# Value columns of two dilated groups by one product of 512 columns, and w_out's second read asked for later

## The chip, the cores and the metric

The kernel runs on one NeuronCore of a Trainium2 chip, as one launch. The metric is the device time of that launch in microseconds (us), the median of a few executions; lower is better. Engines are named as the profile names them: PE is TensorE's matmul, PEld its weight load, DVE VectorE, ACT ScalarE, POOL GpSimd, SP SyncE, which here only asks for transfers. Everything is in float32 unless it says bf16.

## The reference, cut to what matters

One layer of a hybrid decoder for a prompt of 512 tokens and eight sample tokens. The normalised input is multiplied by one wide weight w_in (1024 x 4992), and the columns of the product go to three kinds of heads:

```python
u = rmsnorm(x, norm_mix)                       # (512, 1024) and (8, 1024)
cols = split(u @ w_in, COL_SIZES)              # 4992 columns
aq, af, ai, ag, bq, bk, bv = cols[:7]          # 384 columns each: recurrence (a), differential attention (b)
dil = [cols[7+3*g : 10+3*g] for g in range(3)] # q, k, v of 256 columns for each dilated group
mix = concat(hgrn2(aq, af, ai, ag), diff_attention(bq, bk, bv), combine(dilated(dil, rates=(1, 4, 16))))
h = x + mix @ w_out
h = h + moe(rmsnorm(h))                        # top group of 4, two of its 4 experts
y = rmsnorm(h + sigmoid(rmsnorm(h) @ pgw) * (p @ ppw))
```

In groups 1 and 2 a token attends to tokens 4 or 16 places apart, so their values are wanted in an order in which the tokens with the same remainder modulo 4 stand together.

## The kernel before

The input, transposed, lies in `xT`: 128 partitions x 8 blocks of the 1024 features x 520 tokens. w_in is read in 13 slabs of 384 columns (1.5 MB each) into two buffers in the tile `EXPERT`, in the order of the constant `ORDER` (0, 1, 2, 4, 5, 6, 7, 9, 11, 8, 3, 10, 12). Slab 10 is the twelfth and lies in buffer 1, slab 12 is the last and lies in buffer 0. `projection_units` cuts every slab into units. A unit is one accumulation over the 8 feature blocks into one of two PSUM banks, which take turns (`ps[:, u % 2]`), and a copy by ACT:

- FM ("feature major"): 128 columns of w_in are the weights of the array, 512 tokens stream through: 8 products of 512 columns (L2184).
- TM ("token major"): 128 tokens of `xT` are the weights, the slab's columns stream through: 384 of them for slabs 2, 3 and 6, 256 for the values in slabs 8, 10 and 12 (L2189). For slabs 10 and 12 `cols` picks every fourth token, so the weights are read from `xT` with a step of four elements.
- SM: the slab's 384 columns for the eight sample tokens (L2195).

A float32 product shows as two records, here called passes: 8 products are 16 passes. `schedule` cuts each unit into four pieces, of two feature blocks and so four passes each (32 for SM), and writes one list of steps that all engines walk through in the same order, each doing its part. From slab 7 on the pieces are woven into the differential attention as work for PE between its steps: 24 rounds n (6 heads in each of 4 blocks of queries), with `d_s(n)` (scores), `d_t(n-1)` (transposes) and `d_pv(n-2)` (times values), and 1.7 pieces behind every step. Between them a round passes through DVE and ACT: DVE takes the largest score (L1645), ACT the exponentials of two maps (L1176), DVE weighs them (`weigh`, L1657 to L1660), then PE transposes (L2282), ACT copies (L1186) and PE multiplies by the values (L2294). On DVE's list `weigh(n-1)` stands ahead of the maximum of round n. Between the rounds also stand work for the sample tokens (`dec_q`, `dec_new` on DVE) and the gates (`gate_fn` and others). After the rounds the dilated attention begins with `c_s(0)` (L2312, L2314; maximum L1668), with `mtp(0, .)` and `dec_soft` behind it, and the first product by w_out, `wop(0, 0, 0)` (L2459).

SP asks for all transfers in list order: a slab is asked for when the slab two before it has been used up (`load_slab`, L730). w_out is read in three parts. Part 1 (rows 3 to 5 of 8, 1.5 MB) goes into slab buffer 1 and was asked for once slab 10 was used up; part 0 (rows 0 to 2) goes into buffer 0 and is asked for when all units are done and part 1 has landed; part 2 comes later. `wop(0, 0, 0)` waits for part 1, `wop(0, 0, 1)` for part 0 as well. `cached(b, kv)` reads pages of the cache, and waits until DVE has used the buffer; `outputs` stores values; `reload` reads rows of x again.

The mixture of experts then reads 48 weight blocks of 2 MB through nine slots, and the last part is the per-layer input gate (L2732).

Of the kernel before, what the change touches and what calls it, by code (L numbers as in the profile page):

```python
# [15 lines left out]
ACT = mybir.ActivationFunctionType  # L16
AX = mybir.AxisListType

P = 128
D = 1024  # L20
DC = D // P
SEQ = 512
NT = SEQ // P
# [3 lines left out]
SLAB = 384  # L27
NSLAB = N_IN // SLAB
# [49 lines left out]
ORDER = (0, 1, 2, 4, 5, 6, 7, 9, 11, 8, 3, 10, 12)  # L78
# [5 lines left out]
def projection_units():  # L84

    units = []
    for s in ORDER:
        col = s * SLAB
        if s < 7:
            kinds = ("FM", "FM", "TM", "TM", "FM", "FM", "TM")[s]  # L90
            if kinds == "FM":
                units += [("FM", s, c * P, P, (s, c)) for c in range(3)]
            else:
                units += [("TM", s, 0, SLAB, (s, i)) for i in range(NT)]
        else:
            g, half = divmod(col - C_COL, 768)
            if half == 0:
                units += [("FM", s, c * P, P, (7 + g, c)) for c in range(3)]
            else:
                units += [("FM", s, 0, P, (7 + g, 3))]  # L100
                units += [("TM", s, P, 2 * P, (7 + g, i)) for i in range(NT)]

        units.append(("SM", s, 0, SLAB, None))
        units[-1], units[-2] = units[-2], units[-1]
    return units


def unit_marks(units):

    last = {sl: max(u for u in range(len(units)) if units[u][1] == sl) for sl in range(NSLAB)}  # L110
    summed = {units[u][1]: u for u in range(len(units)) if units[u][0] == "SM"}
    return last, summed
# [14 lines left out]
def schedule(units):  # L127

    last, summed = unit_marks(units)
# [3 lines left out]
    def project_one():  # L133
        u, c0, c1 = todo.pop(0)
        steps.append(("proj", u, c0, c1))
        at = ORDER.index(units[u][1])
        if u == last[units[u][1]] and c1 == DC and at == NSLAB - 2:
            steps.append(("w_out_load", 1))
        if u == last[units[u][1]] and c1 == DC and at + 2 < NSLAB:
            steps.append(("slab", at + 2))  # L140
            if at < 8:
                steps.extend([("copy", 1 + x, at) for x in range(2)])
            elif at < 10:
                steps.extend([("copy", 0, 4 * (at - 8) + x) for x in range(4)])
# [55 lines left out]
    c = []  # L200
# [13 lines left out]
    stop = len(units)  # L214
# [129 lines left out]
def hybrid_kernel(nc, a, o):  # L344
    ctx = ExitStack()
    with ctx:
        def sb(name, shape, dt=F32):
            return ctx.enter_context(nc.sbuf_tensor(name, shape, dt))
# [9 lines left out]
        EXPERT = sb("EXPERT", [P, 2 * CAPW])  # L358
# [10 lines left out]
        cvT = EXPERT[:, at0:at0 + NT * NG * 256].rearrange("p (g i n) -> p g i n", g=NG, i=NT)  # L369
# [15 lines left out]
        xT = sb("xT", [P, DC, NTOK])  # L385
# [28 lines left out]
        ps = ctx.enter_context(nc.psum_tensor("ps", [P, 8, 512], F32))  # L414
# [81 lines left out]
        S_ = {n: sem(n) for n in names}  # L496
# [127 lines left out]
        NU = len(UNITS)  # L624
        LASTU, SUMU = unit_marks(UNITS)
# [14 lines left out]
        def cols(ap):  # L640
            return ap.rearrange("p (s r) -> p r s", r=4)
# [72 lines left out]
        def _(sp):  # L714
            for i in range(NT + 1):
                src = a["x_prompt"][0, i * P:(i + 1) * P, :] if i < NT else a["x_sample"].rearrange("b t d -> (b t) d")
# [84 lines left out]

            def w_out_load(part):
                if part == 1:
                    sp.wait_ge(S_["unit_pe"], 1 + LASTU[ORDER[NSLAB - 2]])
                    dst, src = EXPERT[:, 3 * D:6 * D], wo[:, 3:6]
                elif part == 0:
                    sp.wait_ge(S_["unit_pe"], NU)
                    sp.wait_ge(S_["woload"], 16)
                    dst, src = EXPERT[:, 0:3 * D], wo[:, 0:3]
                else:  # L810
                    sp.wait_ge(S_["c_s_pe"], NCU // 2)
                    sp.wait_ge(S_["kr_pe"], SOFT_KR)
                    dst, src = EXPERT[:, 8 * D:10 * D], wo[:, 6:8]
                sp.dma_start(dst.rearrange("p (c n) -> p c n", n=D), src).then_inc(S_["woload"], 16)
# [96 lines left out]
            for i in range(T5):  # L911
                src = a["p_prompt"][0, 0, i * P:(i + 1) * P, :] if i < NT else a["p_sample"][0].rearrange("b t d -> (b t) d")
# [132 lines left out]
        def _(act):  # L1045
            n = [0]
            s = nc.scalar
# [31 lines left out]
            def proj(u, k0, k1):  # L1079
                kind, sl, c0, w, at = UNITS[u]  # L1080
                if k1 < DC:
                    return
                act.wait_ge(S_["unit_pe"], u + 1)
                src = ps[:, u % 2, :]
                scale = 1.0
                if kind == "TM" and at == (2, 0):
                    act.wait_ge(S_["tab_ok"], 1)
                if kind == "FM" and at == (9, 0):
                    act.wait_ge(S_["s_o_pe"], 1)
                if kind == "SM":  # L1090
                    for q in range(4):
                        at_ = sl * SLAB + q * QSL
                        last = s.activation(samp[:, at_:at_ + QSL], src[32 * q:32 * q + NS, 0:QSL], ACT.Copy)
                    last.then_inc(S_["unit_ok"], 1)
                    return
                elif kind == "TM":
                    g, i = at
                    dst = iT[:, i] if g == 2 else gT[:, i] if g == 3 else bvT[:, i] if g == 6 else cvT[:, g - 7, i]
                    src = src[:, 0:w]
                else:  # L1100
                    g, c = at
                    if g < 2:
                        dst = aF[:, g, c, 0:SEQ]
                    elif g < 7:
                        dst, scale = dF[:, g - 4, c], SCALE_B if g == 4 else 1.0
                    else:
                        dst, scale = cF[:, g - 7, c], SCALE_C if c < 2 else 1.0
                        if g > 7:
                            dst, src = dst.rearrange("p (r s) -> p r s", r=4), cols(src)
                s.activation(dst, src, ACT.Copy, scale=scale).then_inc(S_["unit_ok"], 1)  # L1110
# [1046 lines left out]
        def _(pe):  # L2157
            t = nc.tensor
# [3 lines left out]
            for i in range(NT + 1):  # L2162
# [4 lines left out]
                for c in range(DC):  # L2167
                    last = t.transpose(ps[:, 2 + 2 * (i % 2) + c // 4, (c % 4) * P:(c % 4) * P + r],
                                       XM[0:r, i, c * P:(c + 1) * P], ident[0:r, 0:r])
                last.then_inc(S_["xt_pe"], 1)  # L2170
            pe.wait_ge(S_["xt_ok"], 2 * NT)

            def proj(u, k0, k1):
                kind, sl, c0, w, at = UNITS[u]
                at_ = ORDER.index(sl)
                W_ = slab[at_ % 2]
                if k0 == 0:
                    pe.wait_ge(slabload[at_ % 2], 16 * (at_ // 2 + 1))
                if k0 == 0 and u >= 2:

                    pe.wait_ge(S_["unit_ok"], u - 1)
                for c in range(k0, k1):
                    if kind == "FM":
                        last = t.matmul(ps[:, u % 2, :], W_[:, c, c0:c0 + w], xT[:, c, 0:SEQ],  # L2184
                                        start=(c == 0), stop=(c == DC - 1))
                    elif kind == "TM":
                        i = at[1]
                        rows_ = cols(xT[:, c, 0:SEQ])[:, i] if at[0] > 7 else xT[:, c, i * P:(i + 1) * P]
                        last = t.matmul(ps[:, u % 2, 0:w], rows_,  # L2189
                                        W_[:, c, c0:c0 + w], start=(c == 0), stop=(c == DC - 1))  # L2190
                    elif kind == "SM":
                        if u == SUMU[ORDER[0]] and c == 0:
                            pe.wait_ge(S_["xt_ok"], 2 * (NT + 1) + 1)
                        for q in range(4):
                            last = t.matmul(ps[32 * q:32 * q + 32, u % 2, 0:QSL], xS[:, c, :],  # L2195
                                            W_[:, c, q * QSL:(q + 1) * QSL], start=(c == 0), stop=(c == DC - 1))
                if k1 == DC:
                    last.then_inc(S_["unit_pe"], 1)
# [381 lines left out]
            for k in range(T5):  # L2580
                last = t.matmul(ps[:, 6, T5 * NE:(T5 + 1) * NE], onesb, C[:, k], start=(k == 0), stop=(k == T5 - 1))
            last.then_inc(S_["rank_pe"], 1)
            pe.wait_ge(S_["rank_ok"], 1)
            for i in range(T5):
                for k in range(2):
                    last = t.matmul(ps[:, 2, 0:1], R0[:, i], partsb[:, i, k:k + 1], start=(i + k == 0), stop=(i + k == T5))
# [75 lines left out]
            for m in range(2 * T5):  # L2662
                for k in range(2):
                    last = t.matmul(ps[:, 6, 96:96 + MAXT], Rsel[:, m], Tsel[:, m, k], start=(m + k == 0),
                                    stop=(m + k == 2 * T5))
# [109 lines left out]
```

## Time and profile before

| | us |
|---|---|
| Median of 3 runs | 952.28 (952.0 to 952.67) |
| The profiled execution's own time | 947.98 |
| Its span, first to last instruction | 946.2 |
| PE busy | 883.3 (93%) |
| PEld busy | 469.5 (50%) |
| DVE busy | 385.5 (41%) |
| ACT busy | 240.0 (25%) |
| Mean granted TensorE clock | 0.971 |

Times in the views count from the span's start. "Busy" of PE is modelled: passes overlap in the records, so the spacing of their starts, which the chain of waits gives, is the better measure of what a pass costs. A half under PEclk means 1.2 GHz in place of 2.4.

### The profile page before, as it was taken

Reading aid. Unit: us, or ns where it says so; the run is one execution under the profiler, and the core shown is the slowest. Engines: PE = TensorE matmul, PEld = TensorE weight load, DVE = VectorE, ACT = ScalarE, POOL = GpSimd, SP = SyncE. Lnnn points to the kernel's source line nnn. Section 1 sums busy time; section 2 is a strip of 40 time slices with the busy share of each in tenths; the row PEclk is TensorE's granted clock in tenths of the full one; section 3 lists DMA queues with packets and bytes.
Section 4 is the critical chain, followed back from the end, with each engine's and each line's share of the span. In section 5 each row is a group of like instructions: output and inputs, shape, how many; then the busy total and the mean of one; then the engine's idle time right before and its main releaser. Section 6 shows DMA issues by size and latency. Waiting matters only on the chain.

```text
span 946.2 us, 15732 instructions
## 1 busy us (share of the span) xinstructions
PE 883.3 (93%) x6377; PEld 469.5 (50%) x6377; DVE 385.5 (41%) x840; ACT 240.0 (25%) x609; POOL 94.2 (10%) x128
## 2 busy tenths in 40 slices
PE   6999999999999999999989975999999969989995
PEld 3455555655547567766545652443343323333442
DVE  5217455464226566454346567111111111112453
ACT  4144222220223343343222440100000000013354
POOL 1000000000006465000000001000000000002100
PEclk9999999999999999998999996999999999999998
DMA  7664344044437765243475367999999999994111
GB/s 233 236 253 157 68 156 156 1 156 176 163 110 260 254 209 160 71 153 108 146 231 201 121 237 266 375 410 395 379 401 401 385 382 426 377 373 136 48 45 46
DMA packets 70339, 209.56 MB, mean 221 GB/s; under 512 B 18633, under 2 KB 50356, under 8 KB 61692
## 3 DMA queue, kind: packets, MB, share of 16 engines
q1 hardware_dynamic: 55840, 183.40, 52.4%
q0 software_dynamic: 4736, 16.89, 5.3%
q10 hardware_dynamic: 9692, 8.26, 2.7%
q8 instruction: 51, 0.84, 0.4%
q14 instruction: 20, 0.16, 0.0%
HBM read 189.09 MB, written 38.26 MB: 240 GB/s over the span
## 4 chain that ended last, share of the span: by engine, by line
PE 78%; DMA 8%; DVE 7%; ACT 3%; SPq 2%; issue 2%; ACTq 0%; DVEq 0%
PE ps L2184 18%; PE ps L2189 11%; PE ps L2609 10%; PE ps L2732 6%; PE ps L2646 5%; DMA aF<-in_moe_w_up 4%; PE ps L2459 3%; DMA EXPERT<-in_moe_w_up 3%; PE ps L2605 2%; PE ps L2221 2%; PE ps L2571 2%; PE ps L2267 2%; PE ps L2195 1%; PE ps L2348 1%; PE ps L2294 1%
## 5 line engine op out<-in xcount | busy, mean ns | idle before, releaser
L2184 PE MATMUL ps<-xT,EXPERT 128*128 128x512 f32 x384 | 175.0, 600 | 0.5 <-DVE xT L1468 0.5
L2189 PE MATMUL ps<-EXPERT,xT 128*128 128x384 f32 (+1 forms) x384 | 118.9, 451 | 0.0
L2184 PEld LDWEIGHTS ps<-xT,EXPERT 128*128 128x128 f32 x384 | 69.6, 190 | 74.0 <-issue 70.7
L2189 PEld LDWEIGHTS ps<-EXPERT,xT 128*128 128x128 f32 x384 | 77.5, 236 | 21.7
L2086 DVE TENSOR_TENSOR dF<-dF,ps 64x512 f32<-64x512 f32 (+1 forms) x24 | 14.4, 601 | 158.6 <-ACT dF L1364 158.6
L2732 PE MATMUL ps<-EXPERT,xT 128*128 128x512 f32 x128 | 56.0, 594 | 1.3 <-DVE xT L2139 1.3
L2609 PE MATMUL ps<-EXPERT,wk 128*32 128x512 f32 x384 | 47.3, 639 | 8.5 <-DMA EXPERT<-in_moe_w_up 8.3
L1368 ACT ACTIVATE dF<-ps 128x256 f32<-128x256 f32 (+1 forms) x24 | 8.4, 349 | 161.0 <-PE ps L2629 158.1
L1645 DVE TENSOR_REDUCE small<-ps 128x2 f32<-128x256 f32 (+3 forms) x24 | 19.8, 824 | 62.4 <-PE ps L2270 62.4
L2459 PE MATMUL ps<-EXPERT 128*128 128x512 f32 x96 | 44.0, 596 | 0.9 <-ACT EXPERT L1280 0.9
L2646 PE MATMUL ps<-EXPERT,dF 128*32 128x512 f32 x384 | 43.6, 594 | 0.5 <-issue 0.5
L1176 ACT ACTIVATE wk<-ps,small 128x128 f32<-128x128 f32 (+3 forms) x48 | 24.9, 523 | 74.7 <-DVE small L1645 73.0
L979 POOL TENSOR_TENSOR aF<-aF 128x384 f32<-128x384 f32 x16 | 16.5, 1063 | 271.9 <-DMA aF<-q_d 271.9
L2732 PEld LDWEIGHTS ps<-EXPERT,xT 128*128 128x128 f32 x128 | 23.9, 190 | 29.8 <-issue 28.2
L1110 ACT ACTIVATE EXPERT<-ps 128x384 f32<-128x384 f32 (+2 forms) x36 | 17.6, 490 | 70.0 <-PE ps L2184 35.1
L2096 DVE COPY wk<-ps 128x512 f32<-128x512 f32 (+1 forms) x24 | 14.5, 603 | 46.5 <-PE ps L2646 40.2
L1605 DVE COPY_PREDICATED wk<-lmask,ps 128x384 f32<-128x384 uint8 x56 | 29.3, 577 | 9.6 <-PE ps L2221 9.3
L2221 PE MATMUL ps<-wk 64*128 64x128 f32 x336 | 26.3, 289 | 5.4 <-DVE wk L1591 5.3
L2221 PEld LDWEIGHTS ps<-wk 64*128 64x128 f32 x336 | 20.9, 187 | 20.1 <-DVE wk L1591 10.8
L2609 PEld LDWEIGHTS ps<-EXPERT,wk 128*32 128x32 f32 x384 | 12.5, 117 | 36.4 <-issue 35.5
L1364 ACT ACTIVATE dF<-ps 64x512 f32<-64x512 f32 (+1 forms) x24 | 12.5, 520 | 62.8 <-PE ps L2609 51.7
L1591 DVE TENSOR_TENSOR wk<-wk,aF 128x192 f32<-128x192 f32 x56 | 17.4, 353 | 23.6 <-ACT wk L1146 23.2
(504 smaller groups left out, 1363.5 us busy)
## 6 DMA issues: line engine op xcount, KB each, us to landing
EXPERT<-in_moe_w_gate SPq DMA_DIRECT2D x11, 2048.0 KB, 16.2
EXPERT<-in_moe_w_up SPq DMA_DIRECT2D x11, 2048.0 KB
EXPERT<-in_moe_w_down SPq DMA_DIRECT2D x11, 2048.0 KB, 16.0
EXPERT<-in_w_in SPq DMA_DIRECT2D x13, 1536.0 KB, 6.5
out_win_sample<-in_cache_win SPq DMA_DIRECT2D x16, 1022.0 KB
xT<-in_moe_w_gate SPq DMA_DIRECT2D x5, 2048.0 KB
aF<-in_moe_w_up SPq DMA_DIRECT2D x5, 2048.0 KB, 24.3
samp<-in_moe_w_down SPq DMA_DIRECT2D x5, 2048.0 KB
```

Of the source, the lines that this page charges most:

```text
L1176: last = s.activation(wk[:, n % 2, m * SEQ:m * SEQ + K], ps[:, 2 + 2 * (n % 2) + m, 0:K], ACT.Exp, bias=negm[:, 2 * (n % 2) + m:2 * (n % 2 ...
L1605: last = v.copy_predicated(att, lmask[:, l - 1].unsqueeze(1).to_broadcast([P, 3, P]), src)
L1645: v.tensor_reduce(negm[:, 2 * (n % 2):2 * (n % 2) + 2], ps[:, 2 + 2 * (n % 2):4 + 2 * (n % 2), 0:K], AX.X, ALU.max, negate=True).then_inc( ...
L2184: last = t.matmul(ps[:, u % 2, :], W_[:, c, c0:c0 + w], xT[:, c, 0:SEQ], start=(c == 0), stop=(c == DC - 1))
L2189: last = t.matmul(ps[:, u % 2, 0:w], rows_, W_[:, c, c0:c0 + w], start=(c == 0), stop=(c == DC - 1))
L2221: last = t.matmul(ps[:, 2 + 2 * (k % 2) + e, c * P:(c + 1) * P], L[h, c, :], R[h, c, :], start=True, stop=True)
L2267: t.matmul(ps[:, 2 + 2 * (n % 2) + m, 0:K], dF[r, 0, c, i * P:(i + 1) * P], dF[r, 1, c, 0:K], start=True, stop=False)
L2459: last = t.matmul(ps[:, bank, :], mixT[i % 2][:, c], wout_[c][:, h * 512:(h + 1) * 512], start=(c == 3), stop=(c == 2))
L2571: last = t.matmul(ps[0:r, 4 + 2 * (i % 2) + hf, :], pTt[i % 2][:, c, 0:r], plp_[:, c, hf * 512:(hf + 1) * 512], start=(c == 0), stop=(c == ...
L2609: last = t.matmul(ps[32 * q:32 * q + 32, bank, :], x[:, at:at + 32], w, start=(c == 0), stop=(c == DC - 1))
L2646: last = t.matmul(ps[32 * q:32 * q + 32, 5 + k, :], hidT[k][:, at:at + 32], w[:, hf * 512:(hf + 1) * 512], start=(f == 0), stop=(f == FC - 1))
L2732: last = t.matmul(ps[0:r, 4 + 2 * (i % 2) + hf, :], hnT[i % 2][:, c, 0:r], ple_[c][:, hf * 512:(hf + 1) * 512], start=(c == 0), stop=(c == ...
```

## The change

Slab 10 loses its four TM units, and the four TM units of slab 12 become units of a new kind, TP. Such a unit takes its moving columns out of both slab buffers: 256 value columns of slab 12 (buffer 0) and 256 of slab 10 (buffer 1), 512 in one product, with the same weights read with a step of four. ACT copies the two halves apart. Slab 10 therefore has to stay in its buffer until the last TP unit, and part 1 of w_out, which overwrites it, is asked for when all units are done, in a place further down the list.

There are 57 units in place of 61. The order at the end becomes: slab 10: SM, FM; slab 12: FM, TP 0, TP 1, TP 2, SM, TP 3 (before: slab 10: FM, TM 0, TM 1, TM 2, SM, TM 3; slab 12 the same).

```diff
--- before.py
+++ after.py
@@ projection_units
                 units += [("FM", s, 0, P, (7 + g, 3))]
-                units += [("TM", s, P, 2 * P, (7 + g, i)) for i in range(NT)]
+                if g == 0:
+                    units += [("TM", s, P, 2 * P, (7, i)) for i in range(NT)]
+                elif g == 2:
+                    units += [("TP", s, P, 2 * P, (9, i)) for i in range(NT)]
@@ schedule
-        if u == last[units[u][1]] and c1 == DC and at == NSLAB - 2:
+        if u == len(units) - 1 and c1 == DC:
             steps.append(("w_out_load", 1))
@@ SP: w_out_load
                 if part == 1:
-                    sp.wait_ge(S_["unit_pe"], 1 + LASTU[ORDER[NSLAB - 2]])
+                    sp.wait_ge(S_["unit_pe"], NU)
                     dst, src = EXPERT[:, 3 * D:6 * D], wo[:, 3:6]
@@ ACT: proj
+                elif kind == "TP":
+                    for k in range(2):
+                        last = s.activation(cvT[:, 2 - k, at[1]], src[:, 256 * k:256 * (k + 1)], ACT.Copy)
                     last.then_inc(S_["unit_ok"], 1)
                     return
@@ PE: proj
+            both = EXPERT[:, 0:2 * DC * SLAB].rearrange("p (k c n) -> p k c n", k=2, c=DC)
...
+                    elif kind == "TP":
+                        last = t.matmul(ps[:, u % 2, :], cols(xT[:, c, 0:SEQ])[:, at[1]], both[:, :, c, P:3 * P],
+                                        start=(c == 0), stop=(c == DC - 1))
```

## Rows read from the trace of the kernel before

**Rows 1.** Windows: stretch, length, busy us per engine, granted clock, DMA share, GB/s.
```profile
337.50:388.60 51.10, 50.03 (x274) 34.78 (x272) 35.63 (x53) 19.65 (x47) 23.03 (x20) 1.00 0.54 175
388.60:413.40 24.80, 24.80 (x197) 21.76 (x197) 14.06 (x35) 9.16 (x25) 0.00 (x0) 1.00 0.04 13
```

**Rows 2.** Timeline of PE: start, us, line, form, idle before and its releaser.
```profile
372.45 0.66 PE L2282 MATMUL ps<-ident,wk 128*128 128x128 f32 x4 [1.07 <-DVE wk L1660]
...
416.22 2.81 PE L2459 MATMUL ps<-EXPERT 128*128 128x512 f32 x6 [0.94 <-ACT EXPERT L1280]
```

**Rows 3.** Chain of waits, 330 to 470: start, us, what, count.
```profile
346.61 2.03 PE ps L2189 x8
...
374.14 1.72 PE ps L2184 x4
...
388.41 0.22 PE ps L2270 x2
...
401.55 0.80 PE ps L2195 x32
...
409.24 0.44 PE ps L2282 x4
...
410.71 1.73 PE ps L2294 x16
412.44 0.65 PE ps L2312 x8
...
413.45 0.70 DVE xT L1668
```

**Rows 4.** Chain of waits, 285 to 330.
```profile
289.93 1.78 PE ps L2189 x8
```

**Rows 5.** Weight loads of L2189, contiguous (288.6) and stepped (346.4): min/median/max ns.
```profile
L2189 PEld LDWEIGHTS ps<-EXPERT,xT x4: 190/190/192, 288.6 to 289.2; 128*128 128x128 f32 x4
L2189 PEld LDWEIGHTS ps<-EXPERT,xT x8: 309/330/332, 346.4 to 348.0; 128*128 128x128 f32 x8
```

**Rows 6.** Timeline of DVE, end of the rounds, and `weigh(14)`.
```profile
339.40 0.62 DVE L1660 SCALAR_TENSOR_TENSOR wk<-wk,small 128x384 f32<-128x384 f32 x1
...
397.24 1.23 DVE L1645 TENSOR_REDUCE small<-ps 128x2 f32<-128x1024 f32 x1 [4.12 <-PE ps L2270]
...
400.96 0.75 DVE L1660 SCALAR_TENSOR_TENSOR wk<-wk,small 128x512 f32<-128x512 f32 x1
```

**Rows 7.** Timeline of ACT, the copy that follows a transpose.
```profile
409.71 0.60 ACT L1186 ACTIVATE PT<-ps 128x512 f32<-128x512 f32 x1 [1.99 <-PE ps L2282]
```

**Rows 8.** Timeline of SP: start, us, transfer.
```profile
337.71 0.39 SPq L730 DMA_DIRECT2D EXPERT<-in_w_in  x1
...
374.18 0.38 SPq L814 DMA_DIRECT2D EXPERT<-in_w_out  x1
...
410.74 0.38 SPq L814 DMA_DIRECT2D EXPERT<-in_w_out  x1
```

**Rows 9.** Landing after the ask: slab 12; the three parts of w_out; all slabs.
```profile
DMA to landing us min/median/max: 8.7/8.7/8.7
...
DMA to landing us min/median/max: 6.4/6.8/7.8
...
DMA to landing us min/median/max: 6.3/6.5/13.8
```

**Rows 10.** Windows around falls of the granted clock.
```profile
431.20:434.60 3.40, 2.08 (x14) 1.31 (x12) 2.58 (x4) 1.74 (x7) 0.00 (x0) 1.00 0.03 10
434.65:441.48 6.83, 6.16 (x38) 5.12 (x39) 3.69 (x12) 2.58 (x9) 0.00 (x0) 0.50 0.18 61
...
489.30:492.70 3.40, 1.53 (x10) 0.77 (x8) 0.80 (x2) 0.87 (x2) 0.00 (x0) 1.00 0.85 266
```

**Rows 11.** Chain of waits at half clock, against L2312 in rows 3.
```profile
436.77 1.16 PE ps L2312 x8
```

**Rows 12.** Waits of PE, 550 to 946: us, times, longest.
```profile
PE ps L2609 <- DMA EXPERT<-in_moe_w_up: 8.3, 2, 7.2
```

More of the change, by code:

```diff
@@ L1093, in proj @@
                         last = s.activation(samp[:, at_:at_ + QSL], src[32 * q:32 * q + NS, 0:QSL], ACT.Copy)
+                    last.then_inc(S_["unit_ok"], 1)
+                    return
+                elif kind == "TP":
+                    for k in range(2):
+                        last = s.activation(cvT[:, 2 - k, at[1]], src[:, 256 * k:256 * (k + 1)], ACT.Copy)
                     last.then_inc(S_["unit_ok"], 1)
```

## Prediction

> **What bounds the kernel now.** I began with the busy shares of the page: PE works 93% of the span, so only what PE does or waits for can count. The change touches the last two slabs, so I read the windows around them [rows 1]. Up to 388.6 us PE is busy 50.03 of 51.10 us, and from there to the start of the dilated attention all 24.80 us. The only wait of the stretch is 1.07 us on `weigh` [rows 2]. PE bounds it, with pieces of the projection between the attention's steps. DVE (14.06 of 24.80 us) and ACT (9.16) have room [rows 1], but by shares alone one would miss that a round passes through them one after the other. I read that next: round 22's maximum starts at 397.24 and its weighing ends at 401.71 [rows 6], so 4.45 us pass before DVE can take the next maximum. A round's own work on PE is d_s 1.28 (1.06 of it scores, 0.22 in the row at 388.41), d_t 0.44, d_pv 0.84 (a half of the 1.73 at 410.71) [rows 3], together 2.56 us. The other 1.9 us of a round are filled by pieces of projection. Where the pieces run out, the bound of a round is the DVE and ACT loop and no longer PE.
>
> After this stretch the order is PE's again; the experts later wait for transfers, 8.3 us in two waits [rows 12]. Their stream of loads starts behind the router, so it moves with whatever comes out here, and I pass the difference on whole.
>
> **The change on PE.** A TM group of 8 passes with stepped weights takes 2.03 us, 0.254 a pass; the same 256 columns with contiguous weights take 1.78 [rows 3, 4]. The loads differ: 330 ns stepped against 190 [rows 5]. So a stepped TM pass is set by its weight load: 0.249 us a pass, and 8 x 0.249 = 1.99 leaves 0.04 for the group. A pass of 512 columns takes 1.72 / 4 = 0.43 [rows 3], longer than 0.249, so its load should hide under the pass before. Only a group's first load shows, behind a short step: a group's cost beyond its loads is 0.04, which is a last pass of 0.213 less 0.17 of overlap with the step before, and for TP the same overlap leaves 0.249 - 0.17 = 0.08. From below that cost is 0, from above 0.14 (the extra 140 ns of the load, [rows 5]). Before: 32 pieces of TM, 32 x 1.015 = 32.5 us. After: 16 pieces of TP, 16 x 1.72 + 10 groups x 0.08 = 28.3 us. PE is spared 4.2 us, and 3.6 to 5.0 between the bounds. If the load added the stepped pass's 0.031 (0.254 - 1.78 / 8) to the 512-column pass too, 64 x 0.031 = 2.0 us less.
>
> Two rules bear on the load. A page of the Trainium skill, "SBUF — State Buffer", in "Door 1: The DMA port swizzle", has a line of 16 bytes and calls a step of up to 4 fp32 free; the load at that very step shows 330 against 190 ns [rows 5], so here it is not free, and by the rule TM passes would cost 0.222, and 128 of them hardly more than 64 of 0.43, which would spare 1 us. Another, "TensorE: Matmul & The Clock Gate", in "Part 3: Packing small matmuls", lets a load overlap a running matmul only where the row groups differ; by it, halving 128 loads of 0.249 would spare 16 us, but the row of 0.254 for a pass whose load alone is 0.249 and whose columns take 0.213 [rows 3, 4] leaves no room for a sum of the two.
>
> **The change in the list.** The pieces woven in are 16 fewer, but each TP piece is longer than the TM piece it replaces (1.72 against 1.02 us), and 1.7 pieces still stand behind each step. So rounds 17 to 21 carry more work, and the last rounds none: the last TP piece stands behind d_s(21), where before pieces reached past d_t(23).
>
> Step 1, to the end of d_s(21), at 388.63 before (388.41 + 0.22, [rows 3]). Work before that point: 19 TM pieces go (19 x 1.02 = 19.4 us); 15 TP pieces come (15 x 1.72 + 9 x 0.08 = 26.5); slab 12's SM comes, two times 0.80 with splits 1.74 [rows 3]; the FM and slab 10's SM are in both, only exchanged. The wait of 1.07 [rows 2] is covered, since more pieces stand ahead of d_t(18). SM now stands where FM covered the gates' SiLU, which makes d_t(14) wait for `weigh(14)`, done at 340.02 [rows 6]: by 337.7 + 0.4 + 1.06 + 0.8 = 339.8 PE is there, 0.2 us. Sum: -19.4 + 26.5 + 1.7 - 1.1 + 0.2 = +8.0 us (+7.3 to +8.6 with the bounds of the first load), so d_s(21) ends at 396.6.
>
> Step 2, from there. Maxima of rounds 21, 22, 23 and their loops: 396.65 + 3 x 4.45 = 410.0 when `weigh(23)` is done. PE meanwhile: last TP piece 1.8 and d_t(20), d_pv(19), d_s(22) to 401.0; d_t(21), d_pv(20), d_s(23) to 403.7; d_t(22) waits to 405.55, 1.9 us; d_t(22), d_pv(21) to 406.9; d_t(23) waits to 410.0, 3.2 us. Then d_t(23) 0.44 [rows 3], ACT's copy 0.60 [rows 7] with d_pv(22) beside it, d_pv(23) 0.84, c_s(0) 1.01 (412.44 to 413.45, [rows 3]) and handovers: 413.0. Before it was 413.45. At full clock the change brings 0.45 us at the point where the dilated attention starts. Bounds: the loop at 4.3 or 4.6 gives or takes 0.45, the first loads 0.7, so -1.6 to +0.7. The two halves of each TP copy on ACT and the four `dec_new` now behind `weigh(23)` (to 412.3) stand beside PE's work and cost nothing; `c_s(0)`'s maximum needs DVE only at 413.0. If the loop were longer, `dec_new` would be late with it.
>
> Step 3, the clock. In the 6.3 us from 403.7 to 410.0 PE works only 1.3. In the trace the granted clock fell to a half behind a stretch of 3.40 us with 2.08 busy, and behind one with 1.53 busy, and stayed there for 6.83 us [rows 10]. At half clock L2312's eight passes took 1.16 in place of 0.65 [rows 11, 3]. So I expect a fall between about 407 and 411. What it costs: nothing while PE waits; from 410.0 up to 2.3 us on d_t(23), d_pv(23), c_s(0); and up to 2.4 on the 2.6 us of `mtp` and `dec_soft`, which at full clock just fit into the 2.77 us from 413.45 to the first product by w_out at 416.22 [rows 2]. Bounds 0 and 4.7. I take 2.0, which is half of some 4 us out of a stretch of 6.83 that lies after 410.0: nearest to the row, since part of the stretch falls into the wait.
>
> Transfers: slab 12 is asked for at 337.7 and took 8.7 us; it is needed now at about 349.5 in place of 374, 3 us after it lands; slabs took 6.3 to 13.8 us [rows 8, 9], so the worst would cost 2. Part 1 of w_out goes out at about 398.4 in place of 374.18, behind `cached(1, 1)` on SP, which then has long gone. Part 0, `outputs` and `reload(0)` are queued behind it; part 0 goes out when part 1 has landed, 398.4 + 6.8 = 405.2, and is there at 412 (410.74 + 6.8 = 417.5 before), 4 us ahead of the need. So all of them are earlier, and no wait that bounds PE is taken away by that.
>
> **Sum.** Against the profiled execution: -0.45 + 2.0 = +1.5 us, 947.98 to 949.5. The median of the runs shown is 4.3 us above that execution; I carry the difference over: 952.28 + 1.5 = 953.8.
>
> **The rivals.**
> - The saving arrives whole: 4.2 of passes and the wait of 1.07, 5 us, 947.3. For it: PE is saturated throughout [rows 1]. It needs a loop of DVE and ACT close to PE's 2.6 us, and rows 6 show 4.45.
> - Slower: a full half-clock stretch lies on the restart. It decides between 410 and 417, where c_s(0), `mtp` and `dec_soft` run at half clock: +4.7 - 0.45, 956.5. It is slower than before as soon as more than 0.45 is lost. For it: the same thing at 434.65 after a shorter lull [rows 10]. Against: the stretch begins in the lull, and some of it passes there.
> - A wash at full clock: the clock stays or falls entirely inside the lull, 951.8. Against it: two lulls in rows 10 with more work in them were followed by a fall.
> - The transfers are late (slab 12 as slow as the slowest, 13.8): 2 us more, 955.8.
> - Loads and passes add up as the page's second rule has it: 64 loads of 0.249 fewer, 16 us, 936. Against: the spacing in rows 3, shown above.
>
> **How the numbers follow.** This kernel's measurement tells 0.2% (1.9 us) from no change. Forecast 0.47, own range 952.4 to 955.4, of which 0.27 lies under the 1.9 us and 0.20 over; slower rival 0.17; wash 0.17, of which 0.03 is faster by more than 1.9; whole saving 0.14; late transfers 0.03; added loads 0.02. Faster 0.19, same 0.41, slower 0.40. Range 949.0 to 956.8: it leaves out most of the whole saving and the tail above the slower rival.
>
> **What would show it.** Right: TP passes 0.43 us apart; two waits of PE on `weigh` of about 2 and 3 us in the last two rounds; c_s(0) starting within 1 us of 412.4; a half under PEclk just after. Wrong: TP passes at 0.46 or more; rounds 21 to 23 at under 4 us; PE waiting for slab 12 or for w_out; the clock at 1.00 through 405 to 417.

## The result and the profile after

| | before | after |
|---|---|---|
| median of the timed runs, us | 952.28 (951.37 to 956.40, 7 runs) | 958.88 (952.28 to 963.12, 7 runs) |
| ratio after / before | | 1.0061, 95% interval 1.0036 to 1.0086 |
| the profiled execution, us | 947.98 | 959.01 |
| its span and mean granted clock | 946.2, 0.971 | 957.2, 0.962 |

The changed kernel is slower by 0.6%. A repetition on another occasion, described below as e11, gave 957.02 us against 953.36, ratio 1.0033 (1.0014 to 1.0053). Both intervals lie above 1. In microseconds they say 3.4 to 8.2 and 1.3 to 5.0 slower. The forecast of 953.8 us (range to 956.8), 1.5 slower, was too low.

**The two waits came.** PE's waits between 330 and 450 us in the trace of after (total, times, longest):

```profile
PE ps L2295 <- DVE wk L1668: 4.8, 3, 2.9
```

L2295 is the transpose of the weights, L2282 before. The timeline of PE shows the three places (start, us, form, idle before and its releaser):

```profile
403.61 0.66 PE L2295 MATMUL ps<-ident,wk 128*128 128x128 f32 x4 [0.18 <-DVE wk L1668]
...
408.05 0.66 PE L2295 MATMUL ps<-ident,wk 128*128 128x128 f32 x4 [1.67 <-DVE wk L1668]
...
412.49 1.12 PE L2295 MATMUL ps<-ident,wk 128*128 128x128 f32 x4 [2.94 <-DVE wk L1668]
```

Before, one wait of 1.07 us stood in this stretch [rows 2]. Now 1.67 us stand ahead of d_t(22) and 2.94 ahead of d_t(23).

**The clock fell in the second one.** The chain of waits of after (start, us, what) from the last TP piece on:

```profile
398.98 1.89 PE ps L2202 x4
...
403.47 1.23 DVE small L1653
...
407.24 0.76 DVE wk L1668
...
411.68 0.76 DVE wk L1668
412.44 0.04 issue
412.49 1.12 PE ps L2295 x4
413.61 3.31 PE ps L2307 x16
416.91 1.16 PE ps L2325 x8
418.07 0.54 PE ps L2327 x2
...
421.41 2.81 PE ps L2472 x6
```

Against [rows 3]: the sixteen products of d_pv took 3.31 us where they took 1.73 (their line was L2294), and the eight of c_s(0) 1.16 where they took 0.65 (L2312). Windows of the same trace (stretch, length, busy us of PE, PEld, DVE, ACT, POOL, granted clock, DMA share, GB/s):

```profile
405.04:408.00 2.96, 1.34 (x7) 0.40 (x6) 2.26 (x7) 1.62 (x5) 0.00 (x0) 1.00 0.56 226
...
409.90:420.10 10.20, 7.61 (x38) 7.19 (x39) 4.48 (x13) 3.01 (x9) 0.00 (x0) 0.50 0.67 254
440.60:454.30 13.70, 13.51 (x60) 7.95 (x59) 4.68 (x14) 2.67 (x9) 0.00 (x0) 0.50 0.32 100
```

The clock is 0.50, the 1.2 GHz level, over 10.2 us that begin in the wait and reach into the work behind it. Before, nothing was at half clock here, and the next stretch was the 6.83 us of [rows 10]. After, that next stretch is 13.7 us long, over saturated PE work.

**The transfers came in time.** SP's timeline of after (start, us of its queue's work, transfer):

```profile
339.28 0.38 SPq L733 DMA_DIRECT2D EXPERT<-in_w_in  x1
...
400.90 6.75 SPq L817 DMA_DIRECT2D EXPERT<-in_w_out  x2
...
419.92 0.34 SPq L825 DMA_DIRECT2D XM<-in_x_prompt  x1
```

Between 330 and 450 us PE never waits for slab 12 or for w_out. The first product by w_out (L2472, 421.41) found it there.

**Where the time of the profiled executions went.** The stretch began 1.57 us later than before (slab 12 asked for at 339.28 against 337.71, [rows 8]), because that execution has a half-clock stretch at 17.3 us that the profiled execution of before lacks. e10 below, a kernel without the TP product, has such a stretch too, and e11, the changed kernel once more, has none, so this isn't of the change. The first product by w_out is later by 421.41 - 416.22 = 5.19 us, 3.62 of them the change's own. It divides as: +0.64 to the end of c_s(0) at full clock; +0.68 (1.12 - 0.44), +1.58 (3.31 - 1.73) and +0.69 (1.70 for c_s(0) against 1.01), together +2.95, for the half clock; +0.03 behind it. The clock's part is a little too large in this sum, and the other too small: the 0.44 us of before is a d_t that follows other work at once, and a d_t after a wait takes 0.66 at full clock as well (e3 below shows one). Against e3, whose clock stayed at 1.00, d_t(23), d_pv and c_s(0) took 1.12, 3.31 and 1.70 in place of 0.66, 1.79 and 0.98, so the half clock cost 2.7 and the change without it 0.9.

Further on, at the chain's `dF` step on DVE, the lag is 8.66 us:

```profile
464.90 0.42 DVE dF L1789
```

That step started at 456.24 in the chain of before. So 3.47 us more came between 421 and 465, where the stretch of 13.7 us lies.

The lull, as the stretch near 410 with its two waits is called below, is best compared between runs by one distance that the early stretch can't touch: from the start of the first d_s to the start of the first product by w_out, on PE's timeline.

| | first d_s | first w_out product | distance, us |
|---|---|---|---|
| before | 237.74 | 416.22 | 178.48 |
| after | 239.31 | 421.41 | 182.10 |
| e11 (after again) | 237.85 | 419.94 | 182.09 |
| e3 (after, PE kept busy) | 239.72 | 419.13 | 179.41 |
| e9 (after by time, TP first) | 239.54 | 415.99 | 176.45 |
| e10 (before by time) | 239.57 | 415.95 | 176.38 |

### The profile page after: what moved, and what is told of

Its sections match the earlier page's. It is cut to its first block, busy times and chain, and to the rows that moved or that the text cites. A ratio compares the mean times of both kernels' runs of the same rounds, so it can differ in the third digit from the quotient of the medians.

```text
span 957.2 us, 15602 instructions
## 1 busy us (share of the span) xinstructions
PE 889.8 (93%) x6313; PEld 462.1 (48%) x6313; DVE 387.3 (40%) x840; ACT 240.0 (25%) x609; POOL 93.8 (10%) x128
## 4 chain that ended last, share of the span: by engine, by line
PE 78%; DMA 8%; DVE 7%; ACT 4%; issue 2%; SPq 2%; ACTq 0%; DVEq 0%
PE ps L2194 18%; PE ps L2622 10%; PE ps L2199 8%; PE ps L2745 6%; PE ps L2659 5%; DMA aF<-in_moe_w_up 4%; PE ps L2472 3%; DMA EXPERT<-in_moe_w_up 3%; PE ps L2202 3%; PE ps L2618 2%; PE ps L2234 2%; PE ps L2584 2%; PE ps L2280 2%; PE ps L2208 1%; PE ps L2307 1%
## 5 line engine op out<-in xcount | busy, mean ns | idle before, releaser
L2199 PE MATMUL ps<-EXPERT,xT 128*128 128x384 f32 (+1 forms) x256 | 82.9, 466 | 0.0
L2745 PE MATMUL ps<-EXPERT,xT 128*128 128x512 f32 x128 | 56.0, 594 | 1.3 <-DVE xT L2147 1.3
L2199 PEld LDWEIGHTS ps<-EXPERT,xT 128*128 128x128 f32 x256 | 46.0, 190 | 21.5
L2472 PE MATMUL ps<-EXPERT 128*128 128x512 f32 x96 | 45.6, 614 | 0.2 <-issue 0.2
L2745 PEld LDWEIGHTS ps<-EXPERT,xT 128*128 128x128 f32 x128 | 23.9, 190 | 29.8 <-issue 28.2
L2202 PE MATMUL ps<-EXPERT,xT 128*128 128x512 f32 x64 | 30.8, 616 | 0.0
L1118 ACT ACTIVATE EXPERT<-ps 128x384 f32<-128x384 f32 (+2 forms) x28 | 14.6, 520 | 61.2 <-PE ps L2194 33.1
```

Source lines behind the costliest of these rows:

```text
L2199: last = t.matmul(ps[:, u % 2, 0:w], rows_, W_[:, c, c0:c0 + w], start=(c == 0), stop=(c == DC - 1))
L2202: last = t.matmul(ps[:, u % 2, :], cols(xT[:, c, 0:SEQ])[:, at[1]], both[:, :, c, P:3 * P], start=(c == 0), stop=(c == DC - 1))
L2472: last = t.matmul(ps[:, bank, :], mixT[i % 2][:, c], wout_[c][:, h * 512:(h + 1) * 512], start=(c == 3), stop=(c == 2))
L2745: last = t.matmul(ps[0:r, 4 + 2 * (i % 2) + hf, :], hnT[i % 2][:, c, 0:r], ple_[c][:, hf * 512:(hf + 1) * 512], start=(c == 0), stop=(c == ...
```

## The experiments

"Half-clock time" below is worked out for each run from its span and mean granted clock, 2 x (1 - clock) x span, and then averaged over the runs of a kernel. The experiments ran in three series, e1 to e4, e5 to e8 and e9 to e11, each beside its own runs of before (35, 35 and 15), and the ratios are to those. In the first series before has 59.1 us of half-clock time. It goes with most of the spread of equal kernels: over the 7 runs of after, 0.51 us of time go with each us of it (correlation 0.96), over the runs of before 0.44, 0.52 and 0.48 in the three series (0.87, 0.92, 0.75). "At full clock" is the mean time less half of it: 924.2 for before in the first series, 924.1 in the second, 924.8 in the third (standard error 0.2 to 0.3 each). It assumes that PE is the bound at half clock, so it flatters a kernel whose half-clock time falls into waits.

**e1_read_late: the kernel before, with only the read of w_out moved.**

```
-        if u == last[units[u][1]] and c1 == DC and at == NSLAB - 2:
+        if u == len(units) - 1 and c1 == DC:
             steps.append(("w_out_load", 1))
...
-                    sp.wait_ge(S_["unit_pe"], 1 + LASTU[ORDER[NSLAB - 2]])
+                    sp.wait_ge(S_["unit_pe"], NU)
```

> The kernel before with one part of the change alone: part 1 of w_out is asked for when all units are done, not when slab 10 is used up; products and their order are those of before. Theory (the lull in the last rounds, and the clock that falls behind it, cost the time): part 0 goes out some 7 us later than now, at about 417, and lands at 424, about when its first product comes (420.7); same within 0.3%, 952 to 955, with a wait on the transfer of 0 to 3 us. Rival (the late read and what is queued behind it on SP cost the time of the change): +4 us or more, 956 to 959.

955.38 us, ratio 1.0038 (1.0011 to 1.0066), half-clock time 58.9: slower by more than the theory's 0.3% and by less than the rival's 4 us. PE's waits, and SP's timeline:

```profile
PE ps L2459 <- DMA EXPERT<-in_w_out: 2.7, 2, 2.0
```

```profile
410.90 6.80 SPq L814 DMA_DIRECT2D EXPERT<-in_w_out  x2
...
425.62 0.50 SPq L822 DMA_DIRECT2D XM<-in_x_prompt  x1
```

In the kernel before, pieces last until 410.9, so the late read costs: PE waits for it, and part 0, the outputs and the reload of `XM` stand in SP's queue behind part 1. In the changed kernel the last piece is done ten us earlier (ask at 400.90, reload at 419.92), and the same edit brings no wait of PE. The two edits of the change are not independent: the early end of the pieces, which makes the lull, also hides the late read.

**e2_lull_before: the kernel before, its pieces handed out faster, so that they run out early.** No TP product.

```
-D_SHARE = 1.7
+D_SHARE = 1.85
```

> The kernel before with pieces of the projection used up faster (1.85 behind each step in place of 1.7), so that the last stands behind d_s(22) and the last rounds have none; no product is changed, no work added or left out. Theory: PE waits on DVE in rounds 22 and 23, some 4 to 5 us in all, nothing is spared elsewhere but the wait of 1.07, the clock falls behind it: +5 to +9 us, 957 to 961. Rival (the 512-column product with stepped weights or the late read is what costs): same as before, within 1 us of 952.3, since pieces only move.

955.34 us, ratio 1.0024 (0.9994 to 1.0055), half-clock time 65.1 (+6.0), at full clock 923.7 (-0.5). One wait of PE instead of two:

```profile
PE ps L2282 <- DVE wk L1660: 3.1, 1, 3.1
```

Its trace is at half clock for 10.2 us from 410.2 on, as that of after. The lull by itself brings the fall and some half-clock time, under half of what the changed kernel has more; whether it brings the time is not settled by an interval that reaches below 1. The expected 957 to 961 was missed: there is one wait of 3.1 us here and not 4 to 5 us in two.

**e3_keep_busy: the changed kernel, with idle products in the two waits.** Two products of 512 columns stand before d_t(22), three before d_t(23); nobody reads what they write.

```
+                if n == NT * HB - 2:
+                    pe.wait_ge(S_["unit_ok"], NU)
+                if n >= NT * HB - 2:
+                    for _ in range(2 + n % 2):
+                        t.matmul(ps[:, 0, :], ident[:], xT[:, 0, 0:SEQ], start=True, stop=True)
```

> The changed kernel with 5 idle-time products added (2 ahead of d_t(22), 3 ahead of d_t(23), each 512 float32 columns, 0.86 us), whose results nobody reads: PE has 4.3 us more work in waits of 2.1 and 2.9 us. Theory: the waits are filled, the clock does not fall at 410, and the kernel gets faster by 3 to 6 us against the changed one although it does more: 952 to 956. Rival (the clock is a by-product and costs nothing): the same as the changed kernel, 958 to 960, or slower.

952.25 us, ratio 0.9981 (0.9955 to 1.0008), half-clock time 55.0. PE's timeline at the same place as in after, with the fillers (L2293):

```profile
406.64 1.94 PE L2293 MATMUL ps<-xT,ident 128*128 128x512 f32 x4
408.47 0.66 PE L2300 MATMUL ps<-ident,wk 128*128 128x128 f32 x4
408.96 1.00 PE L2312 MATMUL ps<-EXPERT,PT 128*128 128x64 f32 x8
409.80 2.79 PE L2293 MATMUL ps<-xT,ident 128*128 128x512 f32 x6
412.91 0.66 PE L2300 MATMUL ps<-ident,wk 128*128 128x128 f32 x4 [0.31 <-DVE wk L1668]
```

```profile
396.00:410.00 14.00, 13.82 (x70) 8.51 (x69) 9.61 (x21) 4.83 (x13) 0.00 (x0) 1.00 0.62 194
410.00:420.00 10.00, 8.75 (x59) 6.05 (x59) 6.43 (x19) 4.38 (x13) 0.00 (x0) 1.00 0.88 323
```

Some 4.4 us of useless work (1.77 + 2.65) took 5 to 7 us off against the two medians of after, which are from other series; the intervals of the ratios (0.9955 to 1.0008 here, 1.0036 to 1.0086 and 1.0014 to 1.0053 for after) don't overlap. d_t(23) starts at the same distance behind the ask for slab 12 (339.69 here: 73.2 us; 73.2 in after), so the DVE and ACT loop sets it in both. What differs is the clock, 1.00 until 420, and d_t(23) takes 0.66 in place of 1.12. The first product by w_out comes 2.7 us sooner after the first d_s than in after, and 0.9 later than before (the table above):

```profile
419.13 2.81 PE L2477 MATMUL ps<-EXPERT 128*128 128x512 f32 x6 [0.94 <-ACT EXPERT L1288]
```

So the kernel only comes back to before: the fillers take the fall away and not the wait.

**e4_share, e5_share_parts, e6_share155_parts: the changed kernel with its pieces spread to the end.** e4 has a share of 1.45 in place of 1.7. e5 has 1.45 too and asks for both parts of w_out at once, on two semaphores, so that part 0 doesn't wait for part 1. e6 is e5 with 1.55.

```
-D_SHARE = 1.7
+D_SHARE = 1.45
...
-            steps.append(("w_out_load", 1))
+            steps.extend([("w_out_load", 1), ("w_out_load", 0)])
```

> The changed kernel with 1.45 pieces behind each step in place of 1.7, so that pieces reach the last round (last behind d_pv(22)). Theory: no wait of PE in the rounds, the 3.5 us that the products spare and the 1.07 us arrive, the clock stays up: 947 to 949, and the start of the first product by w_out some 4 us earlier than before's 416.2, if part 0 of w_out, asked for late, doesn't hold it up: with the ask at about 408 to 410 part 1 lands at 415 and part 0 at 423, a wait of 1 to 3 us on it, then 950. Rival (products or reads cost the time): 957 to 960 as the changed kernel.

> The changed kernel with 1.45 pieces behind each step (the run before this one) and in addition both parts of w_out asked for at once, each with a semaphore of its own, so that SP does not sit out the landing of the first (6.4 us) before it asks for the second, for the outputs and for the rows of x. Theory (with pieces to the last round, what eats the gain is the read of w_out and SP's queue behind it: 2.8 us of waiting for it and the later rows of x): no wait on w_out above 1 us, no wait on weigh, faster than the kernel before by 2 to 5 us, 949 to 952 where that has 954. Rival (a product of 512 columns or the order of pieces costs by itself): no better than with the parts one after the other, ratio 1.002.

> As the last, with 1.55 pieces behind each step: the last piece stands behind d_pv(20), so both reads go out some 6 us earlier, but rounds 22 and 23 have no pieces. Theory: one wait of 2 to 3 us on weigh in the last round, the clock may fall behind it; between the changed kernel and the last one: 951 to 955. Rival (the reads set the time, not the lull): better than the last one.

e4: 955.27 us, ratio 1.0018 (0.9991 to 1.0045), half-clock time 66.6. e5: 952.25, 0.9990 (0.9969 to 1.0011), 61.0. e6: 957.18, 1.0051 (1.0031 to 1.0072), 68.7. All three missed what was expected of them (947 to 949, or 950 with a wait; 949 to 952 and 2 to 5 us under before; 951 to 955). PE's waits in e4, in e5 and in e6:

```profile
PE ps L2472 <- DMA EXPERT<-in_w_out: 2.8, 1, 2.8
```

```profile
PE ps L2471 <- DMA EXPERT<-in_w_out: 2.8, 1, 2.8
```

```profile
PE ps L2294 <- DVE wk L1667: 3.3, 1, 3.3
```

With 1.45 the waits on `weigh` are gone, and the wait on w_out that e1 showed is there in their place, since the pieces end late again. Asking for both parts at once leaves that wait as it was, 2.8 us, because it is for part 1; only what comes after part 1 is asked for sooner. The median is 3 us lower than that of e4, but the intervals of the ratios overlap, the times at full clock are 1 us apart (921.6 and 922.6), and so a gain from it isn't shown. With 1.55 the pieces run out before the last round and a whole lull of 3.3 us is back, with the loss. A share that counts pieces is a coarse handle here, since pieces last from 0.42 to 1.8 us.

**e7_by_time: e5, with the pieces handed out by time.** Each d step adds 1.85 us, and a piece is taken when its own cost is there.

```
+    def cost(u):
+        kind, w = units[u][0], units[u][3]
+        return {"FM": 1.72, "TP": 1.8, "SM": 0.42}.get(kind, 1.35 if w == SLAB else 1.0)
...
-        owed += D_SHARE
-        while todo and todo[0][0] < stop and owed >= 1:
+        owed += D_US
+        while todo and todo[0][0] < stop and owed >= cost(todo[0][0]):
+            owed -= cost(todo[0][0])
```

> The changed kernel with both parts asked for at once, and pieces handed out by their time and not by their number: each step is owed 1.85 us, a piece costs 1.72 (FM), 1.8 (TP), 0.42 (SM), 1.35 or 1.0 (TM). Rounds are filled evenly up to d_t(23). Theory: as the kernel with 1.45 pieces, no wait in the rounds, 949 to 952, if slab 12, asked for later (behind d_pv(13)), still lands in time. Rival (evenness matters, short SM pieces leave rounds of their own open): better than 1.45 by more than 1 us.

949.55 us, ratio 0.9975 (0.9950 to 1.0000), at full clock 919.7 against 924.1: inside the expected 949 to 952, and 2.7 us under e5, as the rival (even filling matters) wanted. Waits left: 2.0 us on w_out and 0.7 on `weigh`.

**e8_busy_twice: e3 with more fillers**, one in `c_pv(1)` and two at the start of `dec_wt`, the sample tokens' weighting, against the half-clock stretch near 440.

```
+                if n == 1:
+                    t.matmul(ps[:, 7, 256:512], ident[:], xT[:, 4, 0:256], start=True, stop=True)
...
+                pe.wait_ge(S_["res_ok"], 1)
+                for _ in range(2):
+                    t.matmul(ps[:, 7, 256:512], ident[:], xT[:, 4, 0:256], start=True, stop=True)
```

> The changed kernel with the idle-time products of the earlier run (5 of 512 columns in rounds 22 and 23) and three more of 256 columns in the second lull, ahead of the wait on ACT's copy in c_pv(1) and of dec_wt, some 20 us after the start of the dilated attention; nobody reads their results. Theory (what a lull costs is the clock that falls behind it): no half stretch near 440, 2 to 3 us faster than with the first five alone, 949 to 951. Rival (the second fall is set by more than the lull): same as with the first five, 952, with the half stretch still there.

954.44 us, ratio 1.0013 (0.9992 to 1.0035): a miss. The stretch near 440 is gone, but the one near 492 is longer, and half-clock time stays at 56.4. Windows, of e8 and then of before:

```profile
492.20:502.40 10.20, 8.67 (x52) 3.74 (x54) 1.40 (x3) 1.08 (x5) 2.31 (x3) 0.50 0.55 192
```

```profile
492.70:499.50 6.80, 6.72 (x40) 2.98 (x44) 1.40 (x3) 1.08 (x5) 2.31 (x3) 0.50 0.76 265
```

Covering one fall moved half-clock time to the next place. At full clock e8 is 926.2, two us above before; the fillers and the wait that stands ahead of two of them are the likely cost, which no run separates.

**e9_tp_first, e10_before_by_time, e11_after_again, side by side.** e9 is the changed kernel with its pieces handed out by time as in e7, with slab 12's TP pieces ahead of its SM and FM, and with part 1 of w_out asked for behind the last TP. e10 is the control for the spacing: the kernel before, by time (1.9 us a step), no TP product, its own reads. e11 is the changed kernel unaltered.

```
+                if g == 2:
+                    units += [("TP", s, P, 2 * P, (9, i)) for i in range(NT)]
                 units += [("FM", s, 0, P, (7 + g, 3))]
...
-                elif g == 2:
-                    units += [("TP", s, P, 2 * P, (9, i)) for i in range(NT)]
...
+def last_tp(units):
...
+    return max(u for u in range(len(units)) if units[u][0] == "TP")
...
-        if u == len(units) - 1 and c1 == DC:
+        if u == last_tp(units) and c1 == DC:
             steps.append(("w_out_load", 1))
```

> The changed kernel with the pieces handed out by time (1.85 us behind each d step) and slab 12's TP pieces taken first, ahead of its SM and FM pieces; part 1 of w_out's second read is asked for when the last TP piece is done and part 0 when all pieces are, so the read is no longer at the very end. Theory (what was left of the loss in e7_by_time was PE's wait of 2.0 us on w_out, and the rest is the clock): no wait of PE on w_out above 0.5 us, none on weigh above 1 us, no half-clock stretch of 10 us at 410, 946 to 949 us, ratio 0.993 to 0.997. Rival (that wait overlaps the stream's end and nothing is left in it, or the clock's later stretches take it): same as e7_by_time, 949 to 951, ratio 0.997 to 0.999.

> Control: the kernel before, without the TP product and with its own reads, only its pieces handed out by time (1.9 us behind each d step) in place of by number. Theory (PE was saturated through the d steps of the kernel before, so spacing alone saves nothing): 952 to 955 us, ratio 0.999 to 1.001. Rival (e7_by_time gained from spacing and not from the product): ratio 0.996 to 0.998, 950 to 951 us.

> The changed kernel unaltered, once more, on the same chip as the other two. Both theories: 957 to 960 us, ratio 1.004 to 1.007; the theory of the clock also wants waits of PE on weigh of 4 to 5 us and a half-clock stretch that begins near 410 us in its profiled run, and a mean half-clock time over its runs some 10 us above that of the kernel before.

| | median us | ratio to before | half-clock time | at full clock |
|---|---|---|---|---|
| before | 953.36 | 1 | 57.9 | 924.8 |
| e9 | 949.29 | 0.9951 (0.9933 to 0.9968) | 58.7 | 919.3 |
| e10 | 950.24 | 0.9966 (0.9952 to 0.9979) | 57.2 | 921.5 |
| e11, after | 957.02 | 1.0033 (1.0014 to 1.0053) | 70.8 | 920.9 |

e10 goes against what I expected, 952 to 955: the spacing alone brings 0.34%, no less than the whole of e7 (0.25%), so e7's gain was no proof for the product. The chain of e10 (L2199 are the xS products, those for the sample tokens), and then the sums of those products, first in before and then in e10, over the stretch from the first d_s to c_s(0):

```profile
402.76 1.46 PE ps L2199 x64
...
412.18 0.65 PE ps L2316 x8
```

```profile
L2195 PE MATMUL ps<-EXPERT,xS 128*32 128x96 f32 x384 | 11.0, 250 | 0.0
...
L2282 PE MATMUL ps<-ident,wk 128*128 128x128 f32 x60 | 10.8, 278 | 1.1 <-DVE wk L1660 1.1
```

```profile
L2286 PE MATMUL ps<-ident,wk 128*128 128x128 f32 x60 | 10.6, 275 | 0.0
L2199 PE MATMUL ps<-EXPERT,xS 128*32 128x96 f32 x384 | 9.8, 248 | 0.0
```

That stretch is 173.56 us in e10 and 175.65 before, 2.1 less: the wait of 1.1 is gone, and the xS products stand together (64 in 1.46 us) where before 32 stood alone (0.80, [rows 3]) between other pieces, 9.8 us in all against 11.0. This accounts for 2.1 of the 3.1 us between the medians; the rest is open.

e9 has the lowest median of all, 0.5% under before, and just misses the expected 946 to 949. The longest wait in its trace between 330 and 450 us:

```profile
PE ps L2304 <- DVE wk L1677: 1.7, 1, 1.7
```

None is on w_out, as expected, but the one on `weigh` is 1.7 us where I had allowed 1: with the TP pieces first, nothing covers the gates' SiLU of slab 12, and the trace falls to half clock there for 3.4 us. Against e10 it is 1 us better by the medians (the intervals overlap) and 2.2 by the times at full clock (standard errors 0.4 and 0.3), which is near the 3.5 us of passes less the 1.7 of that wait. The traces add that the clock takes this back: four passes of 512 columns behind the wait take 3.06 us in place of 1.72, and the first product by w_out comes at the same time in both, in e9 and then in e10:

```profile
415.99 2.81 PE L2481 MATMUL ps<-EXPERT 128*128 128x512 f32 x6 [0.94 <-ACT EXPERT L1297]
```

```profile
415.95 2.81 PE L2463 MATMUL ps<-EXPERT 128*128 128x512 f32 x6 [0.94 <-ACT EXPERT L1284]
```

So by its time no kernel here shows a gain of the product itself that is clear of noise.

e11 repeats the loss, with an interval that overlaps the first one in its lower part. Its trace begins without the early half-clock stretch of after, and so shows the change's own part directly:

```profile
410.22 0.76 DVE wk L1668
...
411.02 1.11 PE ps L2295 x4
412.14 3.31 PE ps L2307 x16
415.44 1.16 PE ps L2325 x8
...
419.94 2.81 PE ps L2472 x6
```

```profile
407.80:418.00 10.20, 7.45 (x39) 6.86 (x38) 5.08 (x15) 3.01 (x8) 0.00 (x0) 0.50 0.74 268
438.50:445.30 6.80, 6.26 (x39) 5.22 (x39) 3.69 (x12) 2.56 (x9) 0.00 (x0) 0.50 0.17 58
```

From the first d_s to the first product by w_out this execution takes 3.61 us more than before (3.62 in after); its stretch at 438.5 is 6.8 us, as long as before, where after had 13.7, and its span was 949.2, 3.0 over that of before. So the loss at 410 is in both executions, and what follows it varies. Runs of this one kernel lie 10 us apart (951 to 961), and their time goes with their half-clock time (correlation 0.95 in e11); where in the span the others had it was not recorded.

## Why the prediction was wrong

**The TP pass: right, 0.7 us too cheap in sum.** The chain of after has the groups

```profile
360.49 1.72 PE ps L2202 x4
...
364.99 3.61 PE ps L2202 x8
...
373.81 3.55 PE ps L2202 x8
...
377.97 1.89 PE ps L2202 x4
```

A pass is 0.43 (1.72 / 4); a group adds 0.11 to 0.17 for its first load, where I took 0.08 with 0.14 as the bound (the 0.08 came from 0.249 and 0.213 us a pass, which no row shows). All 64 passes took 29.0 us in place of 28.3, so 3.5 us were spared and not 4.2, just below my range of 3.6 to 5.0. Their weight loads took

```profile
L2202 PEld LDWEIGHTS ps<-EXPERT,xT x64: 307/308/332, 359.9 to 399.9; 128*128 128x128 f32 x64
```

A load of 308 ns goes under a pass of 430, so the two don't add up to 0.74: the rival with 936 us is out. The Trainium skill's page "SBUF — State Buffer" ("Door 1: The DMA port swizzle") calls a step of up to 4 fp32 free; with 308 ns against 190 for contiguous weights [rows 5] the trace disagrees, and this step's price simply doesn't show behind 512 columns.

**Step 1: right in mechanism, 0.8 us short.** d_s(21) ended at 398.98, less the late start of 1.57 is 397.41, against 396.6. 0.6 of it is the first fifteen TP pieces, 27.1 us in place of 26.5.

**Step 2: right in its waits, 0.5 us short behind them.** Two waits on `weigh`, 1.67 and 2.94 us against 1.9 and 3.2. The loop was 4.44 us from weighing to weighing (407.24 to 411.68) against 4.45. weigh(23) was done at 412.44 - 1.57 = 410.87 against 410.0, the 0.8 of step 1 carried on. From there to the end of c_s(0) I had 3.0 us. At full clock it takes 3.5, as e3 shows: 0.66 for a d_t behind a wait, where I took the 0.44 of a d_t in a full row of work, 1.79 for d_pv(22) and d_pv(23) and 0.98 for c_s(0). So at full clock the change costs 0.9 us (0.6 by the rows of before alone) instead of bringing 0.45: outside the bound of +0.7.

**Step 3 failed, by size.** The fall came where it was expected (409.9, and 407.8 in e11; I said 407 to 411), and e3 shows it as the cause of most of the loss: with PE kept busy and nothing else spared, the slowdown is gone but for 0.9 us at the first product by w_out. Three things were off.

- The term of +2.0 for the clock. It rests on a stretch of 6.83 us with some 4 of it behind the wait. The stretch was 10.2 us in after and in e11, 7.6 of it behind the wait (412.49 to 420.1). Up to the first product by w_out it cost 2.7 us against e3, 2.95 by the rows of before.
- The upper bound of 4.7. I had `mtp` and `dec_soft` just fit into 2.77 us at full clock, but [rows 2] say that PE sat idle for the last 0.94 of them: the work takes 1.83. At the lower clock it took up the idle time and cost nothing (the +0.03 above). By these rows the bound should have been 3.2 (2.3, and 2 x 1.83 less 2.77).
- "I pass the difference on whole". In e11 it was so, 3.6 us at the first product by w_out and 3.0 in the span. In the profiled execution of the first result it was not: the next half-clock stretch grew from 6.8 to 13.7 us and cost 3.47 more.

The sum with what was measured, +0.9 and +2.7 in place of -0.45 and +2.0, is +3.6, 955.9 us. It lies in both measured intervals (3.4 to 8.2 and 1.3 to 5.0). The "slower" rival (956.5) had the mechanism, a half-clock stretch on the restart; its weight of 0.17 was small against two rows of before that both showed a fall behind a lull with more work in it, but its price of +4.7 was too high at that place, and that 956.5 lies close to the measured times is partly luck. That the first median lies another 3 us above the sum goes with half-clock time behind 421 us in the one execution that was profiled; for the other runs it is not shown.

Over the runs the half-clock time is 73.5 us (after) and 70.8 (e11) against 59.1 (the runs of before in the first series) and 57.9 in before, 13 to 14 us more (standard errors 2 to 3), of which the lull's own stretch makes 10.2. At 0.5 us of time for each us that is +7.2 and +6.5, against times at full clock that are 2.5 and 3.9 better than before; the two together are the differences of the means, +4.7 and +2.6 (the medians differ by 6.6 and 3.7). Most of those 2.5 and 3.9 is no gain of the change: the lull's stretch counts for 5.1 us in this measure and cost 2.7 in the trace, so 2.4 of them come from half-clock time that fell into waits.

One sign that I had set was not met: c_s(0) was to start within 1 us of 412.4 and started at 415.3 (416.91 - 1.57), 2.0 of it from the half clock.

**The rivals.** The whole saving is out (PE waited). The wash at full clock is out, since the clock fell; that its 951.8 is close to e3, where the clock stays up, bears out no more than that. Late transfers: none in after; e1 and e4 show that they are the next limit when the pieces last longer.

## What to carry to other kernels

When work is taken from the engine that bounds a kernel, and that work was filling gaps of a loop on other engines, look at where the gaps now open: here 3.5 us fewer passes became 4.8 us of waits and a fall of the granted clock. Spread the filling by its duration and not by its count, which by itself brought 0.34% (3.1 us), where the cheaper product on top of it brought 1 us by the medians, within the noise. And don't take the next fall of the clock for a copy of the last one, in length or in place: compare the half-clock time over several runs beside the trace, and keep in mind that it costs nothing while the engine waits.

## What was not expected of the hardware

- 4.4 us of useless products in two waits made the kernel 5 to 7 us faster (from 957.02 or 958.88 to 952.25).
- Two executions of one kernel, equal to 0.01 us from the first d_s to the first product by w_out, had their next half-clock stretch 6.8 and 13.7 us long, and spans of 949.2 and 957.2 us. One of them also had the early stretch at 17.3 us. What decides between them is open.
- A half-clock stretch of 10.2 us cost 2.7 us, since it began in a wait and ended where the engine had idle time to give.
- Taking one fall away (e8) didn't lower the half-clock time: 55.0 with it, 56.4 without.
